# A depthwise convolution on TensorE by groups of four taps: two channel tiles of four in a two-layer diffusion trunk

## What is computed

```python
q, k, v, a = jnp.split(h @ w_in, [ATT_Q, ATT_Q + ATT_KV, ATT_Q + 2 * ATT_KV], axis=-1)
...                                   # q, k normed, rotated; softmax(q k^T) v per head
glu = a[..., :CONV_CH] * jax.nn.sigmoid(a[..., CONV_CH:])
conv = jax.nn.silu(layer_norm(depthwise_conv(glu, conv_w, conv_b), cn_g, cn_b))
return jnp.concatenate([attn, conv], axis=-1) @ w_out, own_kv

def depthwise_conv(x, w, b):          # CONV_K = 31, same padding, one filter per channel
    y = lax.conv_general_dilated(x, w[:, None, :], window_strides=(1,),
        padding=[(CONV_K // 2, CONV_K // 2)], dimension_numbers=('NWC', 'WIO', 'NWC'),
        feature_group_count=x.shape[-1])
    return y + b
```

## Time and profile before

| | |
|---|---|
| median of 3 runs | 1408.44 us (1406.53 to 1408.91) |
| profiled execution | 1407.16 us, its span 1405.4 us |
| PE busy | 1387.9 us (99% of the span) |
| DVE busy | 982.5 us (70%) |
| ACT busy | 569.4 us (41%) |
| GpSimd busy | 49.0 us (3%) |
| chain that ended last | PE 92%, DVE 4%, ACT 2%, DMA 1% |
| 95 taps at L1117 on DVE | 56.5 us |
| first transposes of the attention (L1677) | start at 387.52 us |
| PE busy from 429 to 445 us | 16.00 of 16 us |
| load of a weight unit, issue to landing | 4.9 us (median) |
| SP's loads of weight units near the stage | issued at 372.89 and 381.76 us |

### The profile page before, as it was taken

The page is one execution under the profiler, slowest core; times in us unless marked ns, Lnnn a source line. Parts: engine busy times, 40 slices in busy tenths (PEclk is TensorE's granted clock), DMA queues, the critical chain, the costliest instruction groups (busy, mean ns, idle before and its releaser), DMA issues.

```text
span 1405.4 us, 21243 instructions
## 1 busy us (share of the span) xinstructions
PE 1387.9 (99%) x8109; PEld 1353.9 (96%) x8109; DVE 982.5 (70%) x1507; ACT 569.4 (41%) x800; POOL 49.0 (3%) x54
## 2 busy tenths in 40 slices
PE   7999999999999999999999999999999999999999
PEld 6999999999958999999999999999999999999999
DVE  5788879849896988888238887896464588444432
ACT  4433332236586643333236333322355363333320
POOL 0000000010001200000001000000110010000000
PEclk8999999999999999999999999999999999999999
DMA  9765567533301466654434655674332253343331
GB/s 377 309 232 210 209 238 261 189 120 104 124 1 60 166 227 228 229 225 150 134 136 179 236 213 213 231 245 147 122 148 98 91 206 123 125 141 137 135 121 73
DMA packets 46085, 243.00 MB, mean 173 GB/s; under 512 B 5584, under 2 KB 8272, under 8 KB 25424
## 3 DMA queue, kind: packets, MB, share of 16 engines
q1 hardware_dynamic: 45744, 242.16, 47.6%
q10 hardware_dynamic: 288, 0.13, 0.0%
HBM read 240.57 MB, written 1.70 MB: 172 GB/s over the span
## 4 chain that ended last, share of the span: by engine, by line
PE 92%; DVE 4%; ACT 2%; DMA 1%; issue 0%; SPq 0%; DVEq 0%; ACTq 0%
PE ps L1351 30%; PE ps L1353 29%; PE ps L1352 29%; DVE conv L1117 1%; DVE w_lo L839 1%; DVE n_full L917 1%; PE ps L1654 1%; DMA w_raw<-in_w_units 1%; DVE a_lo L925 0%; PE ps L1792 0%; PE ps L1428 0%; ACT w_hi L518 0%; DMA x<-in_x_cols 0%; DVE smax L1195 0%; PE ps L1412 0%
## 5 line engine op out<-in xcount | busy, mean ns | idle before, releaser
L1351 PE MATMUL ps<-a_hi,w_hi 128*128 128x384 f32 x1616 | 543.8, 337 | 0.8 <-DVE a_lo L925 0.5
L1352 PE MATMUL ps<-a_lo,w_hi 128*128 128x384 f32 x1616 | 540.3, 334 | 0.0
L1353 PE MATMUL ps<-a_hi,w_lo 128*128 128x384 f32 x1616 | 540.3, 334 | 0.0
L839 DVE TENSOR_TENSOR w_lo<-w_raw,w_hi 128x2048 fp32r<-128x2048 f32 x153 | 351.2, 2297 | 196.7 <-ACT w_hi L518 196.7
L518 ACT ACTIVATE w_hi<-w_raw 128x2048 fp32r<-128x2048 f32 x153 | 291.9, 1909 | 250.6 <-DMA w_raw<-in_w_units 250.5
L1351 PEld LDWEIGHTS ps<-a_hi,w_hi 128*128 128x128 f32 x1616 | 303.6, 188 | 7.0 <-issue 3.0
L1352 PEld LDWEIGHTS ps<-a_lo,w_hi 128*128 128x128 f32 x1616 | 303.7, 188 | 0.1
L1353 PEld LDWEIGHTS ps<-a_hi,w_lo 128*128 128x128 f32 x1616 | 303.6, 188 | 0.0
L861 DVE SCALAR_TENSOR_TENSOR m_raw<-m_raw 128x1024 f32<-128x1024 f32 x256 | 299.5, 1222 | 0.0
L1353 PE MATMUL ps<-h_hi,w_lo 128*128 (+1 forms) x704 | 236.6, 336 | 0.0
L1351 PE MATMUL ps<-h_hi,w_hi 128*128 (+1 forms) x704 | 236.5, 336 | 0.0
(11 more groups left out here) (195 smaller groups left out, 834.6 us busy)
## 6 DMA issues: line engine op xcount, KB each, us to landing
w_raw<-in_w_units SPq DMA_DIRECT2D x153, 1024.0 KB, 4.9
m_raw<-in_w_rows SPq DMA_DIRECT2D x128, 512.0 KB, 5.6
m_raw<-in_w_pairs SPq DMA_DIRECT2D x5, 1024.0 KB, 14.1
p_raw<-in_w_pairs SPq DMA_DIRECT2D x3, 1024.0 KB, 25.5
x<-in_x_cols SPq DMA_DIRECT2D x2, 768.0 KB, 5.6
out<-x SPq DMA_DIRECT2D x8, 192.0 KB, 1.9
fourier<-in_k_fourier SPq DMA_DIRECT2D x1, 768.0 KB, 4.4
m_raw<-in_c_ctx SPq DMA_DIRECT2D x1, 512.0 KB, 8.7
```

The lines of the kernel that those rows point to most:

```text
L839: nc.vector.tensor_tensor(w_lo[:, slot(u), :], w_raw[:, slot(u), :], w_hi[:, slot(u), :].bitcast(FP32), ALU.subtract).then_inc(lo_done, 1)
L1351: mm(out, whi, mhi, start=start, stop=False)
L1352: mm(out, whi, mlo, start=False, stop=False)
L1353: return mm(out, wlo, mhi, start=False, stop=stop)
```

## The change

Tiles 0 and 1 stay on DVE with all their taps. Tiles 2 and 3 go to PE. A matmul now takes four taps of 32 channels at once: its 128 lanes of input are the same 32 channels four times, each copy shifted by one more column (`quad_x0`, `quad_x1`), its weights 128x32 (four diagonals of 32 on top of each other: `quad_w0`, `quad_w1`), its output 32 lanes. Four such matmuls, one for each group of 32 channels, are a quad; eight quads (32 taps, the last one zero) are a tile.

- SP copies the shifted rows from `padded`, 16 DMAs of 32 lanes by 427 for each of the two tiles, when the tile is written (`glu_done`), ahead of the load of the mixer's last weight unit.
- GpSimd makes the weights, one product of 128x1024 for each tile, from 32 picked columns of the identity and `quad_wt`, a small array loaded at the start. The second waits until the keys are rotated, since it lies where `rot` was.
- PE does the quads in bank 1 at the places where the diagonal taps were, by the table `QUADS_AT`: four before step 0, then 2, 1, 1, 0, 1, 1, 1, 1, 1, 1, 2, 0.
- ACT no longer makes diagonals. It evicts each tile from bank 1 with its bias at the end of steps 3 and 11 (`QUAD_OUT`).
- DVE does three taps of tile 1 before its last GLU product and two in each step until they are done. It adds the tiles in three sums, into `padded[:, 0]`.
- The scaling stays on ACT, and signals each head apart.

```diff
-DVE_TILES = CT - 1
-DIAGS = 21
-LAST_DVE_TAPS = 6
+DVE_TILES = 2
+QUADS = 8
+GROUPS = 4
...
-            for n in range(5, M0_UNITS):
+            for n in range(5, M0_UNITS - 1):
                 load_unit(u + n)
+            for i in range(CT - DVE_TILES):
+                j = DVE_TILES + i
+                sp.wait_ge(glu_done, j + 1)
+                for g in range(GROUPS):
+                    for k in range(P // COND_GROUP):
+                        sp.dma_start((quad_x0, quad_x1)[i][k * COND_GROUP:(k + 1) * COND_GROUP, g, :],
+                                     padded[g * COND_GROUP:(g + 1) * COND_GROUP, j, k:k + QUAD_N]).then_inc(quad_in[i], 16)
+            load_unit(u + M0_UNITS - 1)
...
+            for i, dst in enumerate((quad_w0, quad_w1)):
+                if i:
+                    pool.wait_ge(quad_ready, 1)
+                    pool.wait_ge(k_roped, 1)
+                nc.gpsimd.tensor_tensor(dst[:].rearrange("p g q c -> p (g q) c"),
...
+            def quad_evict(i):
+                j = DVE_TILES + i
+                act.wait_ge(quad_used, QUADS * (i + 1))
+                nc.scalar.activation(conv[:, j, :], ps[:, 1, 0:CONV_N], ACT.Identity,
+                                     bias=vec_b[:, B_CONV_B + j:B_CONV_B + j + 1]).then_inc(quad_out, 1)
...
-                ins.then_inc(prob_done, 1)
-                k = LAST_DVE_TAPS + DIAGS + m
-                tap_diags(k, min(k + 1, CONV_K))
+                    nc.scalar.activation(probs(m)[:, h, 0:width(m)], probs(m)[:, h, 0:width(m)], ACT.Copy,
+                                         scale=srec[:, n:n + 1]).then_inc(prob_done, 1)
+                if m in QUAD_OUT:
+                    quad_evict(QUAD_OUT.index(m))
...
-                more_taps(5)
+                k = 12 + 2 * m
+                taps(1, min(k, CONV_K), min(k + 2, CONV_K))
...
+            def conv_quads_of(n):
+
+                for k in range(quad[0], quad[0] + n):
+                    i, q = k // QUADS, k % QUADS
+                    if q == 0:
+                        pe.wait_ge(quad_in[i], 16 * GROUPS * (P // COND_GROUP))
+                        pe.wait_ge(quad_ready, i + 1)
+                        if i:
+                            pe.wait_ge(quad_out, i)
+                        else:
+                            pe.wait_ge(glu_done, CT)
+                    for g in range(GROUPS):
+                        ins = mm(ps[g * COND_GROUP:(g + 1) * COND_GROUP, 1, 0:CONV_N], (quad_w0, quad_w1)[i][:, g, q, :],
+                                 (quad_x0, quad_x1)[i][:, g, 4 * q:4 * q + CONV_N], start=q == 0, stop=q == QUADS - 1)
+                    ins.then_inc(quad_used, 1)
+                quad[0] += n
...
+QUADS_AT = [4, 2, 1, 1, 0, 1, 1, 1, 1, 1, 1, 2, 0]
+QUAD_OUT = [3, 11]
```

More of the change, by code:

```diff
@@ L238, in build @@
         qk = sb("qk", [P, QT + 1, TOK], stack=r)
+        q = ExitStack()
+        quad_x1 = sb("quad_x1", [P, GROUPS, QUAD_N], stack=q)
+        q.close()
         qk_sq = sb("qk_sq", [P, QT + 1, TOK], stack=r)
@@ L242, in build @@
         pick_half = sb("pick_half", [P, 2], stack=r)
+        q = ExitStack()
+        quad_w1 = sb("quad_w1", [P, GROUPS, QUADS, COND_GROUP], stack=q)
+        q.close()
         rot = sb("rot", [P, QT + 1, LAT], stack=r)
@@ L317, in build @@
         mix_hi, mix_ready = sem("mix_hi"), sem("mix_ready")
-        diag_ready, tap_used = sem("diag_ready"), sem("tap_used")
+        quad_in = [sem(f"quad_in{i}") for i in range(CT - DVE_TILES)]
+        quad_ready, quad_used, quad_out = (
+            sem(n) for n in ("quad_ready", "quad_used", "quad_out"))
         ln_mean_done, ln_xc, ln_sq, ln_stat, ln_ms, ln_root, ln_diag, ln_bc, ln_y = (
@@ L387, in load_ffn @@
                     load_unit(u0 + 2)
-                    for dst, src in ((vec_b[:], cols_b), (conv_wt[:], conv_cols)):
+                    for dst, src in ((vec_b[:], cols_b), (conv_wt[:], conv_cols), (quad_wt[:], conv_quads)):
                         sp.dma_start(dst, src).then_inc(vectors_in, 16)
@@ L1206, in mix_low @@
                 nc.vector.tensor_tensor(a_lo[:, j, :], src, a_hi[:, j, :].bitcast(FP32), ALU.subtract).then_inc(mix_ready, 1)
[L1208 to L1219, removed]
             split(u + 8)
-            more_taps(6)
+            taps(1, 9, 12)
             glu_mul(3)
@@ L1231, in _ @@
                     attention(m + 1)
-                more_taps(5)
[L1233 to L1239, removed]
+                k = 12 + 2 * m
+                taps(1, min(k, CONV_K), min(k + 2, CONV_K))
+                if m == PAIR_STEPS - 2:
+                    dve.wait_ge(conv_done, DVE_TILES)
+                    a = mark(nc.vector.tensor_tensor(conv_sum(), conv[:, 0, :], conv[:, 1, :], ALU.add))
+                    dve.wait_ge(dve_self, a)
+                    dve.wait_ge(quad_out, 1)
+                    a = mark(nc.vector.tensor_tensor(conv_sum(), conv_sum(), conv[:, 2, :], ALU.add))
             dve.wait_ge(dve_self, a)
-            dve.wait_ge(dve_self, mark(nc.vector.tensor_tensor(conv_sum(), conv_sum(), conv[:, 2, :], ALU.add)))
-            dve.wait_ge(dve_self, b)
-            nc.vector.tensor_tensor(conv_sum(), conv_sum(), conv[:, last, :], ALU.add).then_inc(conv_summed, 1)
+            dve.wait_ge(quad_out, 2)
+            nc.vector.tensor_tensor(conv_sum(), conv_sum(), conv[:, 3, :], ALU.add).then_inc(conv_summed, 1)
             mix_low(QT - 1, ps[:, 0, 0:TOK])
@@ L1421, in mod_columns @@
                 for q in range(PAIR_TILES):
[L1422 removed]
+                    ins = mm(ps[:, 7, 2 * q:2 * q + 2], mod_part[:, k % 2, q * P:(q + 1) * P], mod_pick[:, 0:2], start=True, stop=True)
                 ins.then_inc(cols_done, 1)
@@ L1644, in _ @@
             pe.wait_ge(e_tc, 2)
[L1646 to L1653, removed]
-                    mm(ps[:, 1, 0:CONV_N], tap_diag[:, k % DIAGS, :], padded[:, CT - 1, k:k + CONV_N], start=k == LAST_DVE_TAPS,
-                       stop=k == CONV_K - 1).then_inc(tap_used, 1)
-                    tap[0] = k + 1
+            quad = [0]
+            def conv_quads_of(n):
[13 more added lines that the diff above has]
+                quad[0] += n
             def scores(m):
@@ L1703, in _ @@
             values(PAIR_STEPS - 1)
-            assert tap[0] == CONV_K
+            assert quad[0] == QUADS * (CT - DVE_TILES)
             def means(src, at):
@@ L1857 @@
     named["conv_cols"] = np.ascontiguousarray(np.asarray(inputs["conv_w"])[0].reshape(CONV_K, CT, P).transpose(2, 1, 0))
+    taps = np.zeros((QUADS * 4, CONV_CH), np.float32)
+    taps[:CONV_K] = np.asarray(inputs["conv_w"])[0]
+    quads = taps.reshape(QUADS, 4, CT, GROUPS, COND_GROUP).transpose(1, 4, 2, 3, 0).reshape(P, CT, GROUPS, QUADS)
+    named["conv_quads"] = np.ascontiguousarray(quads[:, DVE_TILES:])
     arrays, args = {}, []
```

43 lines of the change are left out of this document (22 added, 21 removed).

## The result

| | before | after |
|---|---|---|
| median of 6 runs each | 1407.65 us (1405.97 to 1408.91) | 1413.90 us (1411.49 to 1415.16) |
| span of the profiled execution | 1405.4 us | 1412.1 us |
| scores(0) to the projection | 381.66 to 428.99: 47.33 us | 382.89 to 430.55: 47.66 us |
| from the projection to the end | 976.4 us | 981.6 us |

The ratio is 1.0045, with a 95% interval of 1.0033 to 1.0056. The forecast was 1403.9 us and faster; it was wrong. I split the span at two points that both kernels have, the first scores of the attention and the first matmul of the projection. The 6.7 us of the two spans then lie in three places: 1.23 before the stage, 0.33 in it, 5.14 behind it. The prediction spoke of the middle one alone.

What follows compares the result with a forecast made beforehand. DVE's chain, with PE nearly as long, was taken to bound the even layer's attention stage. A 1.4 us loss at the start and 5.9 gained from step 4 made 4.5 net: 1408.44 to 1403.9 us, range 1400.5 to 1407.8.

Steps and rivals of the forecast that it cites:

- PE's work behind unchanged: Sign that the forecast holds: after the attention stage, PE's work stays as it was.
- I take 0.50 and 1.6 ... 384.2.: Stage start: SP's first 16 copies issued 0.50 us apart, landing after 1.6, all there at 384.2; PE waits 1.2 us.
- bounds of 0 to 5.3: Stage start: range in us given for PE's wait for the first 16 copies, with 1.2 taken in the sum.
- PE's clock falls, since PE has more gaps: Rival, chance 0.02: half the stage's matmuls at 1.2 GHz would cost some 9 us, ending near 1409.
- the rival of the late copies: Stage start, chance 0.05: each 0.1 us of spacing costs 1.5 us; at 1.0 spacing the kernel needs about 1411.5.
- The quads: PE in the attention stage: 0.75 us each in a group, 0.80 alone; 12.5 us in all against 19.2 for diagonal taps.
- The serial rival: Chance 0.02: the array's column groups run one after another, quads take 44 us instead of 19, kernel about 1431.
- The lower end of 0.70: PE in the attention stage: us per quad if only the streaming grows from 256 to 399 columns; 0.78 at most.
- The pace from step 4 on: Exponential of step 4 to projection: PE and ACT's round trip, 9.1 us per three steps, 26.7 instead of 32.55, gain 5.9.
- The bounds of 8.5 and 9.7: Period of three steps in us: 8.5 if all waits hide, 9.7 if each handover costs 0.2 more.
- GpSimd: Two weight products, 2.7 us each; the second, near 374.5, slows DVE's split of a weight unit, hidden in DVE's gap.
- the rule that the prediction quoted: A DVE instruction with two SBUF inputs and a GpSimd instruction reading SBUF exclude each other; the split waits some 2.3 us.

Runs made afterwards that it cites:

- a_al_busy: The changed kernel with 32 unused bytes ahead of h_hi and h_lo, plus five matmuls nothing reads ahead of the first quads: 1405.90 us, ratio 0.9993 to before.
- a_al_split: The changed kernel with 32 unused bytes ahead of h_hi and h_lo, its first sixteen copies issued by SP, ACT and GpSimd: 1401.75 us, ratio 0.9968 to before.
- a_al_late: The changed kernel with 32 unused bytes ahead of h_hi and h_lo, and quads ordered later, none before step 0: 1404.44 us, ratio 0.9983 to before.

## Why the prediction was wrong, step by step

**What it left out: the addresses.** The costs were added up for the instructions that the change adds, removes and moves. 2112 matmuls that it doesn't touch became 3 ns slower each, 6.4 us, because new arrays moved their operand. No view of the trace of before could have given this size: nothing there shows the same matmul from two addresses. But the range was built on the sentence "PE's work behind unchanged", and an edit that adds or widens persistent arrays doesn't keep that. With this term alone the 4.5 us of gain would have become a loss of 1.9.

**"I take 0.50 and 1.6 ... 384.2."** This is the step of the sum that failed in the stage. The measured values are 0.634 and 2.0 us, the copies are there at 387.75, 386.5 on the scale of before (the stage begins 1.23 later): 2.3 us late, inside the bounds of 0 to 5.3 that I had given PE's wait, but not in the sum. I took the spacing from four loads from HBM of 64 KB; a copy from SBUF to SBUF of 53 KB has another one, and fifteen times 0.13 make 2.0 us; the landing adds 0.4. I had named a spacing above 0.6 as a sign of being wrong, and it came. The Trainium skill ("DMA: Bandwidth & Descriptors", section "Anatomy of one DMA — SWDGE (gpsimd) path") puts the fixed cost of a DMA at some 2.0 us, mostly the receipt at the target; the median landing of 2.0 agrees with it, though these copies were issued by SP and that section describes GpSimd's.

**"PE's clock falls, since PE has more gaps" at 0.02.** I had argued it for the whole stage, from averages of 10 and 8 us. It fell in one place, behind the one wait that I had forecast myself (1.2 us, in truth 3.73). It cost 1.5 us beyond the 3.0 that I had put for four quads, 1.7 beyond the 2.82 of a full clock, and 1.66 in a_al_busy's comparison. The rival's price was off too: 9 us on 1403.9 make 1413, not the 1409 that I wrote. The rival was named and its place was not: the late copies and the low clock are one event, so that each microsecond of waiting there cost more than one. In the rival of the late copies, "the net gain is gone when the last copy lands at 388.7", the point comes earlier: at 386.5 on the same scale the gain was gone, for the low clock and because the pace from step 4 on gave 1.2 us less than forecast.

**The quads: right.** 0.75 in a group and 0.80 alone were forecast; four take 2.82 (0.70 each), two 1.48 (0.74 each), one 0.81 with the change of form (398.61 to 399.42). The column groups run at the same time, as the row of the first FFN had said. The serial rival is out. The lower end of 0.70, "if only the streaming grows", didn't follow from that row by the prediction's own formula: a quad has two rounds of records, and 143 more columns add 2 x 2 x 143 / 2.4 GHz = 0.24 to its 0.50, so 0.74. The sum didn't use that bound.

**The pace from step 4 on: nearly right.** The exponential of step 4 begins at 402.68, the projection at 430.55: 27.87 us, where 26.7 were forecast and before needed 32.55. A period of three steps (exponential of step 7 to that of step 10, 412.08 to 421.57) is 9.49 us, not 9.1:

```profile
412.08:421.57 9.49, 8.57 (x82) 4.32 (x78) 7.10 (x16) 8.63 (x26) 0.00 (x0) 1.00 0.00 0
```

PE 8.57, DVE 7.10, ACT 8.63: forecast were 8.6, 7.2 and 8.5. The bounds of 8.5 and 9.7 held it. DVE's taps have left the chain, but not all of DVE: its low part, maximum and scaling of the maximum, 1.61 us in a row, still stand in the chain of waits from 401 to 431 us (start, us, what), there and once more at 423.49:

```profile
404.51 0.56 DVE a_lo L1235
405.07 0.88 DVE smax L1224
...
405.97 0.17 DVE smaxn L1226
```

**GpSimd: right in its effect.** The product began at 375.83 and took 1.92 us (2.7 estimated; the first one, begun at 326.54 behind a split of DVE's, took 3.06), DVE's split of a weight unit beside it 3.76 instead of 2.29. POOL and DVE, in that order:

```profile
375.83 1.92 POOL L507 TENSOR_TENSOR quad_w<-mod_pick,quad_wt 128x1024 f32<-128x1024 f32 x1 [46.24 <-DVE qk L1199]
```

```profile
375.61 0.61 DVE L1157 TENSOR_TENSOR padded<-e_sig,ps 128x128 f32<-128x128 f32 x2
376.13 3.76 DVE L868 TENSOR_TENSOR w_lo<-w_raw,w_hi 128x2048 fp32r<-128x2048 f32 x1
379.82 1.97 DVE L1146 SCALAR_TENSOR_TENSOR conv<-padded,conv_wt,conv 128x399 f32<-128x399 f32 x3
383.52 0.62 DVE L1157 TENSOR_TENSOR padded<-e_sig,ps 128x128 f32<-128x128 f32 x2 [1.73 <-ACT e_sig L677]
```

The product ends at 377.75, the split 2.14 later, about its usual length: it seems to have waited for the whole of the product, as the rule that the prediction quoted has it (Trainium skill, "SBUF — State Buffer", "Who interferes with whom"). In a_al_split the product starts at 376.10, and there three taps take 4.05 us instead of 1.97. The GLU product at 375.61 isn't stretched, and DVE still waits 1.73 us ahead of the next one, so all of it is hidden, as forecast. So were the evictions and the moved load: PE is busy for 15.00 of 15 us from 432 to 447.

**The balance.** In after, the copies 2.3 us later than forecast and the low clock 1.5 put step 4's exponential 5.0 us later than before's (402.68 less 1.23, against 396.44), where 1.4 were forecast; from there 4.68 come back, 5.9 were forecast. That is the 0.33 us loss of the stage. With copies in time and `h_hi` in a fast place the same change measures 4.9 us in the median (1401.75 beside 1406.69), 4.5 by the ratio, and 4.83 in the stage. That the forecast of 4.5 is near is luck, since two errors cancel: the start costs nothing when the copies are in time (scores to exponential of step 4 are 14.63 us there, before 14.78), and the pace gives 1.2 less.

## What to carry to other kernels

Look at where the big operands lie after any edit that adds an array: if the unchanged matmuls take a few nanoseconds more each, put some unused bytes in front before judging the edit. Count the issues of small DMAs that one queue makes ahead of PE's first use of them, with a spacing measured for the same form, and share them among the queues that are idle there. A pause of PE like the 3.7 us here is to be priced with the slow matmuls that can follow it; filling it with five matmuls that nothing reads gave some 1.3 us back.

## What the hardware showed that I had not expected

- fp32r matmuls of 128x384 over a moving operand of 33792 bytes a lane took 334 to 336 ns a record where it began 64 to 192 bytes behind a multiple of 256, and 338 to 340 where it began 224, 0 or 32 behind. From start to start that is 70/406 to 70/405 us beside 70/400 to 70/398, 1.2 to 2% where PE is never idle. The weights had not moved. Why it is so is open.
- Issues of copies within SBUF (32 lanes by 427 columns) on SP are 0.634 us apart, 0.591 of it the issue, with a landing of 2.0 us. GpSimd issued four of them in 2.13 us, ACT four in between its own work.
- Two quads behind pauses of 1.9 and 1.0 us (a_al_late) took 2.82 us, four quads behind 3.7 us of waiting 4.4 to 4.5, four without such a pause 2.82. Behind waits of 0.7 to 1.4 us later in the stage the clock stayed full.
